# Two fused transformer blocks in split float32: index heads projected first, a LayerNorm moved from GpSimd to VectorE, and several operations put in another order

## The chip, the cores and the metric

The kernel runs on one core of a Trainium2 chip. The metric is the device time of one launch in microseconds. Engines are named as in the profile: PE is TensorE, DVE is VectorE, ACT is ScalarE, POOL is GpSimd, SP is SyncE, which issues the weight loads. The computation has batch 1 and 256 tokens, so each token tensor is two tiles of 128 partitions, tile 0 and tile 1.

## What is computed

The first block runs twice (layers 0 and 1). Each layer projects the input, selects 64 keys for each query with four small index heads, runs eight-head attention on the selected keys, gates a second half through a causal token mix (whose input `v` goes through GELU and a LayerNorm of its own), and then has an output projection, a feed-forward part and a gated side input `p`.

```
h = x @ w_in[i]                        # 1024 x 2116: q k v | qi ki wi | u | vs
logits = einsum('bqhd,bsd->bqhs', qib, ki);  score = einsum(relu(logits), wib)
_, idx = lax.top_k(score, topk)        # 64 of up to 256 keys
b_out = u * (einsum(w, layer_norm(v)) + b_s)       # u, v after gelu
mix = concatenate([a_out, b_out]) @ w_o[i]
x = layer_norm(ALPHA * x + mix, ln1_g[i], ln1_b[i])
ffn = (silu(gate) * up) @ w_ffn_out[i]
ple = (p[i] @ w_ple[i]) * sigmoid(x @ w_ple_gate[i])
x = layer_norm(ALPHA * x + ffn + ple, ln2_g[i], ln2_b[i])
```

The second block also has two layers (an even and an odd one). Each has an RMS norm with a modulation, a large input projection, two kinds of attention, an output projection gated into x, a second RMS norm with modulation, and a squared-ReLU feed-forward part 1024 x 4096 x 1024.

## The kernel before

A hand-written list fixes the order of everything: `do(part, ...)` appends to `order`, and each engine's program walks the same list and emits its own share of each part. So an engine works strictly in the order of that list, and a wait in one part holds up all that comes later on that engine.

All large matmuls are three matmuls of float32r: a weight piece is split into a high half (`high`, a copy on ACT into another buffer of `WB`) and a low half (`low`, a subtraction on DVE, L1728), and activations are split the same way (`XTH`/`XTL`, `HTH`/`HTL`; the low halves are DVE subtractions, L1733, L1795, L1799, L1823). PE computes high x high (L1415), high x low (L1416) and low x high (L1417). A piece holds up to 2048 columns for each partition: four 128-row steps of 512 columns, or of fewer. One piece is used by both token tiles, that is by 24 matmuls when it has four row steps.

`loads` issues the transfers on SP; `advance()` emits `high` and `low` for pieces until three pieces are ready ahead of PE (`cur["pairs"]`), and `advance(1)` for one. With `cur["lag"]` set, `advance` leaves the low half of the newest piece pending; it is emitted at the next `advance`, at the next call of `lows()`, or when its matmul is emitted. `linear` runs one chunk of weights over both tiles; with `touter=True` tile 0 goes through all its pieces first, and `mid()` is called between the tiles. `linear2` runs two chunks A and B (two pieces each) so that tile 1 may come late: A0 and A1 of tile 0, B0 of tile 0, then A0, A1, B0 of tile 1, then B1 of both. Its `mid()` emits what makes tile 1 ready; it is called after A0 of tile 0 (`mid_at=0`).

`busy(b, pad)` (L1400) lets PE run `pad` matmuls of 512 bf16 columns with results that nobody reads, ahead of a wait. They are called filler matmuls here.

The first block's layer, in order: three chunks of 364 columns (`w_in` columns 0 to 1092) are copied to `H` (`hin`). `rope_in` on DVE rotates the index heads and then the q/k heads of each tile, and duplicates the keys into `KD`. PE transposes nine 128-column blocks of each tile (`turn_T`, L1430), `sel_score` computes the index logits (L1452) and DVE adds them up (L1875). Eight rounds of `sel_round` (MAX8 and MATCH_REPLACE8, L1889 and L1892) and `sel_mask` (L1899) follow, with the two GELU chunks between the rounds. `sgu_ln` is the gated half's LayerNorm: sums on ACT, small values on POOL, the normalised value on ACT, and gain and bias on POOL (L1367, L1371). `p_split` splits the side input on ACT and DVE (L1904). Then `attention` runs six units: `scores` (L1491, mask L1497), `soft` (maxima on DVE L1911, L1921, exponentials on ACT), `turns` (transposes of E, L1430) and `values` (L1515), with a filler generator that gives PE other work in between. The output projection, LayerNorm `ln_tile` (`ln_stats` on DVE, `rsqrt` on POOL L1337 and L1339, `ln_apply` of two 128x1024 instructions on DVE, L1991 and L1994), both halves of `w_ple`, and `w_ple_gate` (a `linear2`) follow.

In the second block `norm_tile` is square sums on ACT, `rsqrt` on POOL and `norm_apply` on DVE (L1999). `modulate` (called `go(t, pad)`) is eight PE transposes and scale and shift on ACT and DVE (L1817), and the split into `XTH` and `XTL` (L1823). `gated_put` (L2078, L2082) adds an output chunk to x on DVE.

## Time and profile before

| what | value |
|---|---|
| median of 3 runs | 1409.96 us (1406.32 to 1410.85) |
| the profiled execution | 1406.22 us |
| its span, first to last instruction | 1404.3 us |
| mean granted TensorE clock | 0.985 |
| PE busy | 1317.6 us, 94% |
| DVE busy | 918.9 us, 65% |
| ACT busy | 658.9 us, 47% |
| POOL busy | 110.8 us, 8% |
| HBM traffic in the first fortieth of the span | 371 GB/s |

All times within the execution are microseconds from the start of the span. Busy time of PE contains its filler matmuls and is therefore an upper bound of its useful work. In a row of the timeline the bracket at the end is the idle time of the engine just before the row, and what ended it. Matmuls overlap in the pipeline, so the time of one is read from start to start.

### The profile page before, as it was taken

What the parts mean: (1) busy time and instruction counts of PE and PEld (TensorE: products, weight loads), DVE (VectorE), ACT (ScalarE), POOL (GpSimd) and SP (SyncE); (2) the same over time, 40 slices, a digit from 0 to 9 for tenths busy, and PEclk for the clock granted to TensorE, in tenths of its full rate; (3) what the DMA queues carried; (4) which work ended last, traced back from release to release, by engine and by line L of the source; (5) the groups of instructions that cost most, each with busy time, mean ns of one, the idle gap of its engine ahead of it and who ended that gap; (6) DMA issues with size and microseconds to landing.
All of it is one profiled execution on the core that took longest, in us unless ns stands there. A gap on an engine that the chain in (4) does not pass through costs nothing.

```text
span 1404.3 us, 16099 instructions
## 1 busy us (share of the span) xinstructions
PE 1317.6 (94%) x6462; PEld 1081.6 (77%) x6492; DVE 918.9 (65%) x1225; ACT 658.9 (47%) x886; POOL 110.8 (8%) x157
## 2 busy tenths in 40 slices
PE   6999999999989999999898898999998969999998
PEld 6767888887967788887698776888876857788886
DVE  4857677766675767775666857766666785654444
ACT  5544533443463544343465454554445544554542
POOL 1020000000020000000214200000003320000000
PEclk9999999999999999999998999999999999999999
DMA  9505588873712668885163203776764420465450
GB/s 371 215 1 210 186 317 312 313 287 120 277 61 75 229 241 311 313 313 202 58 207 112 89 32 142 282 298 252 292 232 153 176 91 1 145 213 182 180 180 30
DMA packets 40361, 270.35 MB, mean 193 GB/s; under 512 B 4560, under 2 KB 4560, under 8 KB 12000
## 3 DMA queue, kind: packets, MB, share of 16 engines
q1 hardware_dynamic: 37712, 259.31, 49.8%
q0 software_dynamic: 2432, 8.98, 1.8%
q8 instruction: 51, 0.84, 0.2%
q10 hardware_dynamic: 144, 1.05, 0.2%
q14 instruction: 22, 0.18, 0.0%
HBM read 268.27 MB, written 1.05 MB: 192 GB/s over the span
## 4 chain that ended last, share of the span: by engine, by line
PE 82%; DVE 10%; ACT 3%; issue 2%; POOL 1%; DMA 1%; SPq 0%; POOLq 0%; ACTq 0%; DVEq 0%
PE ps L1415 24%; PE ps L1417 24%; PE ps L1416 24%; PE ps L1430 5%; PE ps L1515 2%; DVE WB L1728 2%; PE ps L1491 1%; PE ps L1400 1%; DMA RAW<-W 1%; ACT WB L1528 1%; DVE st L1981 1%; DVE X L1991 1%; DVE st L1911 1%; DVE X L1994 1%; ACT E L1528 1%
## 5 line engine op out<-in xcount | busy, mean ns | idle before, releaser
L1728 DVE TENSOR_TENSOR WB<-RAW,WB 128x2048 fp32r<-128x2048 f32 (+4 forms) x210 | 453.4, 2162 | 312.9 <-ACT WB L1528 312.4
L1528 ACT ACTIVATE WB<-RAW 128x2048 fp32r<-128x2048 f32 (+4 forms) x210 | 379.9, 1810 | 232.3 <-PE ps L1417 218.2
L1415 PE MATMUL ps<-WB,XTH 128*128 128x512 f32 (+3 forms) x1176 | 455.4, 387 | 19.6 <-DVE XTL L1733 13.1
L1417 PE MATMUL ps<-WB,XTL 128*128 128x512 f32 (+3 forms) x1176 | 447.3, 380 | 0.0
L1416 PE MATMUL ps<-WB,XTH 128*128 128x512 f32 (+3 forms) x1176 | 447.2, 380 | 0.0
L1415 PEld LDWEIGHTS ps<-WB,XTH 128*128 128x128 f32 x1176 | 223.2, 190 | 61.3 <-DVE XTL L1733 13.4
L1417 PEld LDWEIGHTS ps<-WB,XTL 128*128 128x128 f32 x1176 | 222.6, 189 | 38.3
L1416 PEld LDWEIGHTS ps<-WB,XTH 128*128 128x128 f32 x1176 | 223.0, 190 | 35.7
L1415 PE MATMUL ps<-WB,HTH 128*128 128x512 f32 (+1 forms) x452 | 178.8, 396 | 2.5 <-DVE HTL L1799 2.0
L1417 PE MATMUL ps<-WB,HTL 128*128 128x512 f32 (+1 forms) x452 | 178.4, 395 | 0.0
L1416 PE MATMUL ps<-WB,HTH 128*128 128x512 f32 (+1 forms) x452 | 178.3, 394 | 0.0
L1784 DVE CUSTOM_DVE_ANT_0 RAW<-RAW,cond,colv 128x1024 f32<-128x1024 f32 x96 | 119.3, 1280 | 0.0
L1415 PEld LDWEIGHTS ps<-WB,HTH 128*128 128x128 f32 x452 | 85.1, 188 | 23.0 <-DVE HTL L1799 2.4
L1417 PEld LDWEIGHTS ps<-WB,HTL 128*128 128x128 f32 x452 | 85.1, 188 | 20.1
L1416 PEld LDWEIGHTS ps<-WB,HTH 128*128 128x128 f32 x452 | 85.1, 188 | 19.9
L1337 POOL TENSOR_SCALAR st<-st 128x1 f32<-128x1 f32 (+3 forms) x42 | 23.3, 555 | 976.7 <-DVE st L1984 524.7
L1528 ACT ACTIVATE HTH<-ps 128x512 fp32r<-128x512 f32 (+1 forms) x58 | 32.1, 586 | 138.9 <-PE ps L1430 138.7
L1528 ACT ACTIVATE GB<-ps 128x512 f32<-128x512 f32 (+1 forms) x94 | 46.4, 500 | 90.1 <-PE ps L1417 90.1
L1528 ACT ACTIVATE E<-ps,st 128x128 f32<-128x128 f32 (+1 forms) x104 | 42.5, 420 | 74.7 <-DVE st L1921 74.7
L1400 PE MATMUL ps<-cstb 128*128 128x512 bf16 x198 | 57.0, 398 | 1.8 <-issue 0.2
L1799 DVE TENSOR_TENSOR HTL<-ps,HTH 128x512 fp32r<-128x512 f32 x54 | 35.7, 686 | 32.2 <-ACT HTH L1528 32.2
L1339 POOL TENSOR_TENSOR st<-st,cst 128x1 f32<-128x1 f32 (+3 forms) x42 | 48.2, 1147 | 3.5
(175 smaller groups left out, 989.3 us busy)
## 6 DMA issues: line engine op xcount, KB each, us to landing
RAW<-W SPq DMA_DIRECT2D x220, 1024.0 KB, 5.0
RAW<-W SPq DMA_DIRECT2D x14, 768.0 KB, 4.3
RAW<-W SPq DMA_DIRECT2D x12, 728.0 KB, 5.8
VEC<-vecd POOLq DMA_DIRECT2D x10, 512.0 KB, 7.5
RAW<-W SPq DMA_DIRECT2D x8, 512.0 KB, 3.5
RAW<-W SPq DMA_DIRECT2D x4, 576.0 KB, 3.7
GB<-xTd ACTq DMA_DIRECT2D x1, 1024.0 KB, 8.0
X<-xd SPq DMA_DIRECT2D x1, 1024.0 KB, 17.3
```

The lines of the kernel that those rows point to most:

```text
L1337: eng.tensor_scalar(x, x, scale, eps, ALU.mult, ALU.add).then_inc(*own.up())
L1339: eng.tensor_tensor(x, x, MH.to_broadcast([128, x.shape[1]]), ALU.pow).then_inc(*up("rsqrt", key))
L1400: eng.matmul(banks[b][:, :], identb, cstb[:, 0:512], start=True, stop=True)
L1415: eng.matmul(ps, xh, hi[:, j, c0:c0 + cw], start=first and j == 0, stop=False)
L1416: eng.matmul(ps, xh, lo[:, j, c0:c0 + cw], start=False, stop=False)
L1417: op = eng.matmul(ps, xl, hi[:, j, c0:c0 + cw], start=False, stop=last and j == n - 1)
L1430: op = eng.transpose(banks[b][0:rows, j * 128:j * 128 + 128], src, ident)
L1515: op = eng.matmul(banks[b][:, c0:c0 + dv], PET[:, u["i"], blk * 128:blk * 128 + 128], val, start=(j == 0), stop=(j == len(lst) - 1))
L1528: return eng.activation(dst, src, f, **k)
L1728: eng.tensor_tensor(WB[:, it["raw"], 0:w], RAW[:, it["raw"], 0:w], WB[:, it["high"], 0:w].bitcast(F32), ALU.subtract).then_inc(*up("wl", n))
L1784: op = eng.tensor_tensor_reduce(view[:, q, :], view[:, q, :], cond[:, :], 1.0, colv[:, b0:b0 + 1], ALU.mult, ALU.add, modc[:, it["layer"], ...
L1799: eng.tensor_tensor(HTL[:, r2:r2 + 2, :], banks[b][:, :].rearrange("p (n q) -> p n q", n=2), HTH[:, r2:r2 + 2, :].bitcast(F32), ALU.subtra ...
```

## The change

1. The chunks of `w_in` go in another order and widths: the index columns with wi (768 to 1092, 324 wide) first, then `vs` (512), then q/k/v as 384 and 384, then `u` (512). `rope_in` is cut in two: `rope_sel` (index heads) and `rope_qk`. The index heads are transposed after the first piece of `vs`, scored after its second piece, and the selection rounds run beside the q/k/v chunks. `rope_qk` follows the selection.
2. The gated half's LayerNorm: POOL keeps the small values; gain, bias, mean and root are applied by DVE in two `scalar_tensor_tensor` instructions for each tile (`sgu_apply`). ACT's application and POOL's four are gone.
3. `w_ple`'s first half moves into the attention's filler, ahead of the gating, and its result goes to a place of its own (`PLE`). `p_split` moves up between rounds 3 and 4.
4. The `u` chunk and all until the attention is emitted with `lag` set. The first scores come after q/k are transposed; the wait for the first exponentials has 2 filler matmuls in place of 8.
5. `ln_apply` is cut into `ln_scale`, which does not wait for the root, and `ln_shift`. In places another part stands between them (`halfway`).
6. `mid_at=1` in four of the `linear2` calls (`w_ple_gate`, both input projections of the second block, and `mlp_w1_2`): `mid()` comes after A1 of tile 0. In the second block `gated_put` goes ahead of `modulate`, and the low half of the next piece lags behind it. Between the blocks `norm_sums` brings the root of tile 0 forward, and `modulate` stands between scale and shift of tile 1.

```diff
     for i in range(2):
-        all_rows("w_in", i, 1024, (0, 364), (364, 728), (728, 1092), (1092, 1604), (1604, 2116))
+
+        all_rows("w_in", i, 1024, (768, 1092), (1604, 2116), (0, 384), (384, 768), (1092, 1604))
+        all_rows("w_ple", i, 256, halves[0])
         all_rows("w_o", i, 1024, *halves)
-        all_rows("w_ple", i, 256, *halves)
+        all_rows("w_ple", i, 256, halves[1])
...
+        def ln_tile(key, t, after, between=None, before=None, halfway=None):
             sts, mv = col(12), col(2)
             do("ln_stats", key, t, sts, mv, after)
+            if before:
+                before()
             do("rsqrt", ("ln", key), mv[:, 1:2], 1.0, 1e-5, ("ln_mv", key))
             if between:
                 between()
-            do("ln_apply", key, t, mv)
+            do("ln_scale", key, t, mv)
+            if halfway:
+                halfway()
+            do("ln_shift", key, t, mv)
...
+            def put_sel(t, b, done):
+                put_index(t, b, done)
+                if t:
+                    rope_sel(0)
+
             if i:
-                run(linear2("w_in", "x", xt_w, puts[0:2], mid_in, pad=(6, 0)))
+                fill = linear2("w_in", "x", xt_w, [put_sel, put_gelu(1)], mid_in, pad=(6, 0))
             else:
-                run(linear("w_in", "x", xt_w, puts[0], touter=True))
-                run(linear("w_in", "x", xt_w, puts[1]))
-            run(linear("w_in", "x", xt_w, puts[2]))
...
+                run(linear("w_in", "x", xt_w, put_sel, touter=True))
+                fill = linear("w_in", "x", xt_w, put_gelu(1))
+            next(fill)
+            rope_sel(1)
...
+            tws = []
             for t in range(2):
...
+                tws += turn_T([H[:, t, 768 + j * 128:896 + j * 128] for j in range(2)] + [MIX[:, t, 256:384]],
+                              [("kd", (i, t, 2))] + t_pe, 6, t, pad=0 if t else 2)
+            run(fill)
             for t in range(2):
                 do("sel_start", i, t)
...
+            fill = chain(linear("w_in", "x", xt_w, put_in(1, 0, 384)), linear("w_in", "x", xt_w, put_in(2, 384, 768)))
...
             for rnd in range(8):
+                if rnd % 2 == 0:
+                    next(fill, None)
+                if rnd == 4:
+                    do("p_split", i, list(pt_free))
...
+            for t in range(2):
+                do("rope_qk", i, t, hw[t] + mix_free[t], list(scr["free"]))
+                scr["free"] = [("kd", (i, t, 1))]
+            do("sgu_apply", i, mean, root)
...
+            cur["lag"] = True
+            run(linear("w_in", "x", xt_w, put_gelu(0)))
+            tw = []
+            for t in range(2):
+                tw += turn_T([H[:, t, j * 128:j * 128 + 128] for j in range(4)]
+                             + [MIX[:, t, j * 128:j * 128 + 128] for j in range(2)],
+                             [("kd", (i, t, 1))] + t_pe, 0, t, pad=0 if t else 2)
...
             def gating():
-                yield
                 do("sgw_mask", i)
+                yield from linear("w_ple", "p", [[("pl", i)], [("pl", i)]], put_ple(0))
...
+                    if c and t:
+                        x_n[1] = ln_tile((i, 1, 1), 1, rw[1], halfway=lambda: advance(1))
...
-            attention(units, 0.125, fill, pads=(8,), first=8 if i else 3)
+            attention(units, 0.125, fill, first=3)
...
-            run(linear2("w_ple_gate", "x", xt_w, [put_g(0), put_g(1)], mid1, pad=(0, 3)))
+            run(linear2("w_ple_gate", "x", xt_w, [put_g(0), put_g(1)], mid1, pad=(0, 3), mid_at=1))
...
-                    elif t:
-                        norm_tile(0, x_n[0])
-                        go(0, pad=14)
-
-                x_n[t] = ln_tile((i, 2, t), t, [("add_out", (i, t, c)) for c in range(2)], between)
+
+                before = norm_sums(0, x_n[0]) if t and i else None
+                x_n[t] = ln_tile((i, 2, t), t, [("add_out", (i, t, c)) for c in range(2)], between, before,
+                                 (lambda: go(0, pad=14)) if t and i else None)
...
             def put(t, b, done):
+                gput(t, b, done)
                 if t:
                     go(0)
-                gput(t, b, done)
-                if t:
                     advance(1)
                     norm_tile(1, xg[1])
+
+            cur["lag"] = True
             run(linear(nm_out, "x", xo_w, put, touter=True, mid=lambda: norm_tile(0, xg[0])))
+            cur["lag"] = False
+            lows()
...
             def last(t, done):
-                if t and i == 0:
-                    go(0)
                 for c in range(2):
                     gated_put(i, c, 1, xg)(t, acc4[t][c][0], done[c])
+                    if t and c == 0 and i == 0:
+                        go(0)
...
+            def sgu_apply(i, mean, ss):
+                on.wait_ge(*at("vec2", (i, 2)))
+                for t in range(2):
+                    x = GB[:, t, 512:1024]
+                    on.wait_ge(*at("ln_ss", (i, t)))
+                    on.wait_ge(*at("ln_mean", (i, t)))
+                    eng.scalar_tensor_tensor(out=x, in0=x, scalar=mean[t], in1=VEC[:, 2048:2560], op0=ALU.add,
+                                             op1=ALU.mult).then_inc(*up("sgu_g", (i, t)))
...
+            def ln_scale(key, t, mv):
+                xs, n = X[:, t, :], 3 * (key[1] - 1)
+                on.wait_ge(*at("ln_mv", key))
+                on.wait_ge(*at("vec0", (key[0], n)))
+                eng.scalar_tensor_tensor(out=xs, in0=xs, scalar=mv[:, 0:1], in1=VEC[:, 0:1024], op0=ALU.subtract,
+                                         op1=ALU.mult).then_inc(*up("ln_scaled", key))
```

## Rows read from the trace of the kernel before

**Rows 1.** The page: PE's busy time; the chain of waits by engine, shares.
```profile
PE 1317.6 (94%) x6462; PEld 1081.6 (77%) x6492; DVE 918.9 (65%) x1225; ACT 658.9 (47%) x886; POOL 110.8 (8%) x157
...
PE 82%; DVE 10%; ACT 3%; issue 2%; POOL 1%; DMA 1%; SPq 0%; POOLq 0%; ACTq 0%; DVEq 0%
```

**Rows 2.** Timeline of PE, layer 0: start us, us, instruction, [idle before <-releaser].
```profile
19.34 0.43 PE L1415 MATMUL ps<-WB,XTH 128*128 128x364 f32 x1 [0.78 <-DVE XTL L1733]
...
39.45 0.39 PE L1415 MATMUL ps<-WB,XTH 128*128 128x512 f32 x1
...
44.68 0.39 PE L1417 MATMUL ps<-WB,XTL 128*128 128x512 f32 x1
...
70.36 0.72 PE L1491 MATMUL ps<-T 64*128 64x128 f32 x8 [2.71 <-DVE selb L1899]
...
78.21 1.11 PE L1430 MATMUL ps<-cst,E 128*128 128x128 f32 x4 [2.49 <-ACT E L1528]
...
133.20 1.09 PE L1430 MATMUL ps<-cst,X 128*128 128x128 f32 x8 [0.80 <-DVE X L1994]
...
135.40 0.50 PE L1415 MATMUL ps<-WB,XTH 128*128 128x512 f32 x1 [1.11 <-DVE WB L1728]
```

**Rows 3.** Timeline of PE, layer 1, at the same two waits.
```profile
405.18 0.72 PE L1491 MATMUL ps<-T 64*128 64x128 f32 x8 [1.62 <-DVE selb L1899]
...
413.03 1.11 PE L1430 MATMUL ps<-cst,E 128*128 128x128 f32 x4 [4.11 <-ACT E L1528]
```

**Rows 4.** Windows: PE, PEld, DVE, ACT, POOL busy, then PEclk, DMA, GB/s.
```profile
78.00:82.00 4.00, 3.79 (x17) 3.05 (x18) 1.76 (x5) 2.04 (x11) 0.00 (x0) 0.57 0.02 4
66.98:79.32 12.34, 7.07 (x35) 3.87 (x35) 8.55 (x23) 9.66 (x29) 7.82 (x12) 0.82 0.12 43
```

**Rows 5.** Timeline of DVE, first block, layer 0.
```profile
16.48 1.68 DVE L1728 TENSOR_TENSOR WB<-RAW,WB 128x1456 fp32r<-128x1456 f32 x1 [2.13 <-ACT WB L1528]
18.07 1.22 DVE L1733 TENSOR_TENSOR XTL<-GB,XTH 128x1024 fp32r<-128x1024 f32 x1
...
40.85 0.32 DVE L1834 TENSOR_TENSOR SCR<-H,COS 128x160 f32<-128x160 f32 x1
...
42.27 0.24 DVE L1834 TENSOR_TENSOR SCR<-H,COS 128x80 f32<-128x80 f32 x1
...
49.95 1.51 DVE L1875 SCALAR_TENSOR_TENSOR SCR<-E,H,SCR 128x128 f32<-128x128 f32 x4 [1.57 <-ACT E L1528]
...
54.08 0.62 DVE L1889 MAX8 st<-SCR 128x8 f32<-128x128 f32 x2
...
70.07 0.43 DVE L1899 TENSOR_SCALAR selb<-SCR 128x128 bf16<-128x128 f32 x2
...
73.87 1.60 DVE L1904 TENSOR_TENSOR PTL<-T,PTH 128x512 fp32r<-128x512 f32 x1 [3.37 <-ACT PTH L1528]
...
119.58 1.28 DVE L1991 SCALAR_TENSOR_TENSOR X<-X,st,VEC 128x1024 f32<-128x1024 f32 x1 [1.02 <-POOL st L1339]
```

**Rows 6.** Timeline of POOL, second block: one of the rsqrt instructions.
```profile
869.60 0.98 POOL L1337 TENSOR_SCALAR st<-st 128x1 f32<-128x1 f32 x1 [8.48 <-ACT MIX L1528]
```

**Rows 7.** Timeline of DVE at the same moment.
```profile
868.24 2.29 DVE L1728 TENSOR_TENSOR WB<-RAW,WB 128x2048 fp32r<-128x2048 f32 x1
```

**Rows 8.** Timeline of PE at the four norm-and-modulate places of the second block.
```profile
684.58 1.09 PE L1430 MATMUL ps<-cst,MIX 128*128 128x128 f32 x8 [3.31 <-DVE MIX L1999]
...
689.11 0.58 PE L1415 MATMUL ps<-WB,XTH 128*128 128x384 f32 x1
...
694.53 1.10 PE L1430 MATMUL ps<-cst,MIX 128*128 128x128 f32 x8 [2.46 <-DVE MIX L1999]
...
872.06 1.10 PE L1430 MATMUL ps<-cst,MIX 128*128 128x128 f32 x8 [2.34 <-DVE MIX L1999]
...
1066.35 1.09 PE L1430 MATMUL ps<-cst,MIX 128*128 128x128 f32 x8 [3.51 <-DVE MIX L1999]
...
1215.84 1.09 PE L1430 MATMUL ps<-cst,MIX 128*128 128x128 f32 x8 [2.32 <-DVE MIX L1999]
```

More of the change, by code:

```diff
@@ L707, in put_in, with put_gelu, put, rope_sel @@
                 return put
-            puts = [put_in(c, a, b_) for c, (a, b_) in enumerate(((0, 364), (364, 728), (728, 1092)))]
+            gw = [[], []]
+            def put_gelu(c):
+                def put(t, b, done):
+                    do("gelu", (i, c, t), t, c, b, [done] + gb_free)
+                    gw[t].append(("gelu", (i, c, t)))
+                    give(b, ("gelu", (i, c, t)))
+                return put
+            def rope_sel(t):
+                do("rope_sel", i, t, hw[t] + mix_free[t], list(scr["free"]))
+                scr["free"] = [("kd", (i, t, 2))]
@@ L795, in program, with put_ple, put @@
             sgo = ("gated", (i, 1))
+            def put_ple(c):
+                def put(t, b, done):
+                    do("ple", (i, c, t), t, c, b, [done] + pt_free)
+                    give(b, ("ple", (i, c, t)))
+                return put
             rw = [[], []]
@@ L832, in program @@
             xt_w = xt_n
-            for c in range(2):
-                def put(t, b, done, c=c):
-                    do("ple", (i, c, t), t, c, b, [done, sgo])
-                    give(b, ("ple", (i, c, t)))
-                run(linear("w_ple", "p", [[("pl", i)], [("pl", i)]], put))
+            run(linear("w_ple", "p", [[("pl", i)], [("pl", i)]], put_ple(1)))
             def mid1():
@@ L1106, in program @@
                 run(weave(chain(linear2("odd_w_in_2", "x", xt_w, [put_H("odd", c, c * 512, c * 512 + 512, dw[c])
-                                                                  for c in range(2)], mid, pad=(11, 0)), part((3, 4))),
+                                                                  for c in range(2)], mid, pad=(11, 0), mid_at=1), part((3, 4))),
                           [[ch[0, 0][0]], [gs[0], ch[0, 1][0], ch[0, 0][1]], [gs[1], ch[0, 1][1], ch[1, 0][0]],
@@ L1621, in sgu_ln @@
                         ).then_inc(*up("ln_ss", (i, t)))
-                for t in range(2):
-                    on.wait_ge(*at("ln_nb", (i, t)))
-                    act(GB[:, t, 512:1024], GB[:, t, 512:1024], ACT.Identity, bias=nb[t], scale=ss[t]
-                        ).then_inc(*up("ln_x", (i, t)))
             def p_split(i, after):
@@ L1854, in rope_in, with rope_qk @@
                                   ).then_inc(*up("wi", (i, t)))
+            def rope_qk(i, t, after, free_):
+                for e in after + free_:
+                    on.wait_ge(*at(*e))
                 h3 = H[:, t, 0:640].rearrange("p (h d) -> p h d", d=64)[:, :, 0:16]
-                rope(h3.rearrange("p h (a f) -> p h a f", a=2), cs, sn, 10, 8).then_inc(*own.up())
+                rope(h3.rearrange("p h (a f) -> p h a f", a=2), twice(COS[:, t, 0:8]), twice(SIN[:, t, 0:8]), 10, 8
+                     ).then_inc(*own.up())
                 on.wait_ge(*own.at())
@@ L1961, in gating @@
                 on.wait_ge(*at("gating", (i, gh)))
+                for t in range(2):
+                    on.wait_ge(*at("gelu", (i, 0, t)))
                 for gg in range(4):
```

99 lines of the change are left out of this document (37 added, 62 removed).

## The prediction, made before the changed kernel was run

> **What bounds the kernel now.** I read the page first: PE is busy 94% of the span and 82% of the chain of waits, DVE 10% [rows 1]. So the kernel ends when PE has done its matmuls, and another engine costs time only where PE stands. Then I read PE's timeline for places where it waits or runs filler matmuls. Outside the weight matmuls there are about fifty, mostly under a microsecond. The large ones the change touches are these.
>
> - Selection to attention, in both layers of the first block: PE waits 2.71 us for the selection mask and 2.49 us for the first exponentials, besides its filler matmuls [rows 2]; in layer 1 it is 1.62 and 4.11 [rows 3]. The whole stretch from the last projection matmul to the end of the first transposes of E is 12.3 us [rows 4].
> - LayerNorm ahead of `w_ple_gate`: 0.80 and 1.11 us, in layer 0, with as much again in layer 1 [rows 2].
> - The second block's norms: 3.31, 2.46, 2.34, 3.51 and 2.32 us [rows 8].
>
> The clock matters too: in the 4 us after the long stand at the exponentials it was granted 0.57 [rows 4], so 1.2 GHz for most of that stretch, which about doubles the matmul time in it.
>
> PE's weight work stays. Three chunks of 364 become 324 + 384 + 384, again 1092 columns and the same number of matmuls. A piece of 512-column matmuls takes 5.5 us: 24 of them, 5.23 us from the first start to the last [rows 2], or 0.228 us each. For 324 and 384 columns I scale that by columns with a small fixed part: about 0.150 and 0.175 us each, so 3.6 and 4.2 us for a piece of 24.
>
> **The first block, part by part.**
>
> *Start of layer 0.* Tile 1's low half is queued on DVE behind the low half of the third piece, 1.68 us, and takes 1.22 [rows 5]; PE starts tile 1 at 19.34 [rows 2]. The third piece is now `vs` with 2048 columns: low half 1.68 x 2048/1456 = 2.36 (+0.6), its high half on ACT about +0.5, and 136 KB more to load before it, 0.4 us at the 371 GB/s of this part of the span. PE starts tile 1 some 1.5 us later.
>
> *Index heads.* PE must wait for `rope_sel` of tile 1 after only one `vs` piece. That rope stands on DVE behind a low half of 2048, the rope of tile 0 and a low half of 1536. One 2048 low half is 2.29 [rows 7], 1536 scales to 1.7; the q/k rope of ten heads takes 1.42 from start to start [rows 5], the index one of five heads with its copies at most that, I take 1.0. So 2.3 + 1.0 + 1.7 + 1.0 = 6.0 us, of which the `vs` matmuls (2.7 us in layer 1's order, up to 5.5 in layer 0) and the time until the high half is made cover a part. I price 2.5 us per layer; the bounds are 0 and 5.
>
> *Selection.* Beside it PE now has q/k/v and `u`: 4 x 4.2 + 2 x 5.5 = 27.8 us, and 1.9 for 12 transposes and 2 filler matmuls. On DVE stand: adding the logits 54.08 - 49.95 = 4.1; the eight rounds, 70.07 - 54.08 = 16.0 less the three low halves between them (6.9), 9.1; mask 0.4; four low halves 2 x 1.7 + 2 x 2.3 = 8.0; `p_split`, 1.60 in its row, which I take as 0.7 (below); `rope_qk` 2.8 [rows 5]. That is 25.1: the q/k transposes don't wait. Then `sgu_apply`, four instructions of 512 columns, half of a 1.28 us one each [rows 5], 2.7 with gaps, a low half of `w_ple` (1.2) and DVE's copy of the transposed q/k (0.7). DVE ends at 29.7 + about 0.5 for the relu, PE at 29.7 + copy. A wait of about 1.5 us before the first scores is left, mostly inside the 3 filler matmuls.
>
> By the timelines laid side by side, the first scores of layer 0 then start at about 71.5 where they started at 70.36: the start (1.5), the index wait (2.5) and the copy (1.5) eat the 3.4 us of the mask wait and the 1.5 us of fillers, 1.1 later net. In layer 1, without the start, they come at the same 405.2. What is won is behind them: 8.96 us from scores to the end of the first transposes (70.36 to 79.32) become scores 1.1, scores 1.1, two fillers 0.5 and transposes 0.5 = 3.2, with `w_ple`'s 12 matmuls (2.7, moved, counted below) as cover for the exponentials. That is 5.8, and about 1.1 more because the slow stretch behind it goes. DVE has two low halves and the mask of the mixing weights (1.2) ahead of the second maxima; I take 1.0 off for it. Net: layer 0 5.8 + 1.1 - 1.0 - 1.1 = 4.8; layer 1 5.9.
>
> *Taking 2.7 us of `w_ple` from the stretch ahead of `w_ple_gate`.* It covered DVE's work on LayerNorm. The 0.80 and 1.11 us waits and 0.7 of fillers go, but A1 of tile 0 now needs a low half that lies between `ln_scale` and `ln_shift`, and 4 filler matmuls stand ahead of the transposes without use. I come to 2.0 us regained of the 2.7: -0.7 per layer.
>
> *`ln_scale` ahead of the root.* Before, DVE stood 1.02 us for POOL's root [rows 5]. But a POOL instruction that usually takes 0.19 took 0.98 and ended at 870.58, just after the DVE subtraction of two SBUF operands ended at 870.53 [rows 6, 7]. `ln_scale` has two SBUF operands as well and starts at the moment POOL wants to start. So POOL's root slides behind it and `ln_shift` waits: I count 0 for the split, with 0.95 at each of six LayerNorm tiles on PE's path as the upper bound. The Trainium skill, "SBUF — State Buffer", section "SBUF: two separate sides", says the same as a rule: the port pair shared by VectorE and GpSimd is locked for a whole instruction, by a VectorE one with two SBUF inputs as well. By the rule the split gives nothing where it stands alone; without it the sum would be 3 to 5 us better. It is also why I take `p_split` at 0.7: in its row POOL's gain and bias ran beside it, and they are gone.
>
> **The second block.** A `linear2` with `mid_at=1` covers tile 1's norm with A1 (2.7 us at 512 columns, 2.1 at 384), but leaves only B0 (2.7; 1.6 for 288 columns) between the transposes and A0 of tile 1; that path takes about 3.3 us (689.11 - 684.58 less 1.1 of transposes is 3.4 [rows 8]), so some 0.6 comes back.
> - Between the blocks: tile 0's root no longer stands behind that of tile 1; its transposes start about 1.8 earlier, and without the 3.31 us stand no fillers at half clock follow. With tile 1: 2.4 us won.
> - Even layer's feed-forward: `gated_put` first and the low half deferred bring the norm of tile 1 forward about 1.5, but the deferred low halves and two 1.28 us modulation sums now stand ahead of tile 1's split. DVE becomes the bound: 0.4 won.
> - Odd layer's input: 2.2. Odd feed-forward, the same without the modulation sums: 2.4.
>
> **Sum.** 4.8 + 5.9 - 1.4 + 2.4 + 0.4 + 2.2 + 2.4 = 16.7 us against a span of 1404.3 (device time 1406.22 with 1.9 around it). The work was laid out by hand without the hops between engines at the new waits, so I take 15. The profiled execution lies 0.3% under the median; I subtract from the median: 1409.96 - 15 = 1395.0 us.
>
> **Rivals.**
> - *As computed*, 1389 to 1400: chance 0.55.
> - *DVE binds at more places than the one*: the index wait is nearer 5 than 2.5 in each layer, and the low halves deferred in the second block stand in front of the splits at three places rather than one. Costs 5 + 3: 7 won, 1403. For it: DVE is already the releaser of nearly every wait of PE. Against: it idles about a third of the span [rows 1]. 0.18.
> - *The lock doesn't hold, and slow-clock stretches go that I left standing*: split 4 us, clock 3 to 6: 1385 to 1388. Of the clock: a stand of 2.49 us was followed by a slow stretch [rows 2, 4], and transposes and fillers behind the 3.31 us stand took 4.5 us [rows 8]; small shifts can go either way. 0.10. The split alone would give 1395 - 4 = 1391, which counts with the first case. That would go against the rule of the Trainium skill's page named above.
> - *Within 0.3%*: the pieces cancel, as the first scores already do: start 1.5, index wait 5, no gain from the norms. 1409.96 - 3: 1407. 0.10.
> - *Slower*: with `lag`, low halves are emitted right behind the maxima of a unit and ahead of the next unit's. In each of the 12 units of the two attentions the exponentials could be 2.3 us late and PE with them, up to 27 us. It decides from 1.6 us a unit on, where it has eaten the 19 us beyond which the time is slower by more than 0.3%; full size 1420. Against: the attention had `lag` before, and only two more low halves fall into it. 0.07.
>
> **Range and chances.** 1384 to 1408 holds the first four cases and cuts most of the last and the outer part of the others. About 0.3% (4.2 us) is what a measurement can tell from no change. Faster by more: 0.55 + 0.18 + 0.10 = 0.83 less a little for the tail of the second, 0.82; within 0.11; slower 0.07. The first case's own range is 1389 to 1400.
>
> **What would show it.** After: no wait for `selb` and only a short one for E at the first unit; PE standing 2 to 3 us at the transposes of the index heads (MIX or H from DVE) in both layers; tile 1 starting near 21 rather than 19.34; `ln_shift` following `ln_scale` with a gap of about a microsecond, and the POOL scaling lengthened to over 1 us beside `ln_scale`; in the second block transposes without a wait for L1999's instruction, but short waits for XTL after B0. The prediction is wrong if the index wait exceeds 5 us, if waits for E appear at the later units, or if new slow stretches stand where the clock was full.

## The result: 24.7 us won, 15 forecast

| kernel | median us | runs | profiled execution | span | clock |
|---|---|---|---|---|---|
| before | 1410.24 | 1406.32 to 1410.85 (4) | 1406.22 | 1404.3 | 0.985 |
| changed | 1385.53 | 1384.38 to 1386.78 (4) | 1386.78 | 1385.0 | 0.984 |

The ratio is 0.9831, 95% interval 0.981 to 0.9852. The forecast was 1395.0 with a range of 1384 to 1408 and 0.82 on faster. The time lies in the range, below the first case's own 1389 to 1400.

The two traces differ by 19.3 us of span, the two medians by 24.7. The 5 us between are no row's: before was profiled at the lower end of its runs (1406.22, median 1410.24), the changed kernel at the upper end of its own. What the sum forecast is to be held against 19.3, and the sum was 16.7. (Below, PE "stands" where it waits, and a stretch is "at half clock" where the granted clock is near 0.5, that is 1.2 GHz. The forecast had 0.55 on 1389 to 1400; 1385.5 lies 3.5 us below that.)

First the page of the changed kernel: busy times, then the chain of waits by engine.

```profile
PE 1313.3 (95%) x6436; PEld 1079.2 (78%) x6467; DVE 921.2 (67%) x1233; ACT 654.2 (47%) x882; POOL 110.8 (8%) x145
...
PE 82%; DVE 11%; ACT 3%; issue 2%; DMA 1%; POOL 1%; SPq 0%; DVEq 0%; ACTq 0%; POOLq 0%
```

Beside [rows 1] no engine's busy time moved by more than 5 us. PE has 26 instructions fewer, all of them fillers (198 before, 172 after). The span became 19.3 us shorter and PE's busy time 4.3: for the most part PE stands less. Where, the timeline of PE tells. Layer 0 of the first block:

```profile
20.80 0.64 PE L1445 MATMUL ps<-WB,XTH 128*128 128x324 f32 x1 [2.62 <-DVE XTL L1759]
...
32.34 0.44 PE L1460 MATMUL ps<-cst,H 128*128 128x128 f32 x2
...
70.36 0.71 PE L1521 MATMUL ps<-T 64*128 64x128 f32 x8 [0.18 <-issue]
...
75.40 0.60 PE L1460 MATMUL ps<-cst,E 128*128 128x128 f32 x4
...
126.77 0.77 PE L1445 MATMUL ps<-WB,XTH 128*128 128x512 f32 x1 [2.60 <-DVE WB L1754]
...
131.85 1.04 PE L1460 MATMUL ps<-cst,X 128*128 128x128 f32 x8
```

Neither the mask nor the exponentials are waited for. The first scores start at 70.36, to the hundredth where they started in [rows 2]; the end of the first transposes of E is 76.00, after 79.32, with the 12 matmuls of `w_ple` done on the way. In return a wait of 2.60 us stands at 126.77, where 0.80 and 1.11 stood. Layer 1 (beside [rows 3]):

```profile
358.51 0.44 PE L1460 MATMUL ps<-cst,H 128*128 128x128 f32 x2 [0.35 <-DVE MIX L1877]
...
361.15 0.44 PE L1460 MATMUL ps<-cst,H 128*128 128x128 f32 x2 [2.10 <-DVE MIX L1877]
...
400.77 0.71 PE L1521 MATMUL ps<-T 64*128 64x128 f32 x8 [0.18 <-issue]
```

And the second block, to be read beside [rows 8]:

```profile
672.49 1.09 PE L1460 MATMUL ps<-cst,MIX 128*128 128x128 f32 x8 [0.72 <-DVE MIX L2052]
...
679.68 0.41 PE L1445 MATMUL ps<-WB,XTH 128*128 128x384 f32 x1 [1.20 <-DVE WB L1754]
...
686.00 0.41 PE L1445 MATMUL ps<-WB,XTH 128*128 128x384 f32 x1 [1.06 <-DVE XTL L1849]
...
863.24 0.47 PE L1445 MATMUL ps<-WB,XTH 128*128 128x512 f32 x1 [0.96 <-DVE XTL L1849]
...
1048.45 0.47 PE L1445 MATMUL ps<-WB,XTH 128*128 128x512 f32 x1 [1.19 <-DVE WB L1754]
```

Of the five waits of 2.3 to 3.5 us for `norm_apply` one of 0.72 is left. A short one for a low half (WB) or a split (XTL) stands in the place of the others, 5.1 us in all for 13.9.

Reading the start of the same matmul in both timelines gives the account by stages. "Won" is what the distance grew by within the stage. "Gate stretch" is all from the output projection `w_o` on: LayerNorm, `w_ple`, `w_ple_gate` and the feed-forward part up to its output transposes; what changes in it lies around `w_ple_gate`.

| stage, to the start of | before | after | won | forecast |
|---|---|---|---|---|
| layer 0, `w_o` | 105.01 | 100.68 | 4.3 | 4.8 - 2.7 = 2.1 |
| layer 0 gate stretch, to the output transposes | 331.78 | 326.23 | 1.2 | 2.0 |
| layer 1, first scores | 405.18 | 400.77 | -1.1 | 0 |
| layer 1, `w_o` | 439.68 | 431.10 | 4.2 | 5.9 - 2.7 = 3.2 |
| layer 1 gate stretch | 666.36 | 656.87 | 0.9 | 2.0 |
| between the blocks | 718.95 | 705.88 | 3.6 | 2.4 |
| even feed-forward (848.59 to 835.30 at its head) | 1044.44 | 1029.29 | 1.9 | 0.4 |
| odd input | 1112.84 | 1095.73 | 2.0 | 2.2 |
| odd feed-forward | 1388.21 | 1368.86 | 2.2 | 2.4 |

They sum, with 0.2 in the stage ahead of the even feed-forward's head, to 19.3. The 2.7 is `w_ple`'s half, done in the attention and missing behind it.

### The profile page after: what moved, and what is told of

Its sections match the earlier page's. It is cut to its first block, busy times and chain, and to the rows that moved or that the text cites. A ratio compares the mean times of both kernels' runs of the same rounds, so it can differ in the third digit from the quotient of the medians.

```text
span 1385.0 us, 16064 instructions
## 1 busy us (share of the span) xinstructions
PE 1313.3 (95%) x6436; PEld 1079.2 (78%) x6467; DVE 921.2 (67%) x1233; ACT 654.2 (47%) x882; POOL 110.8 (8%) x145
## 4 chain that ended last, share of the span: by engine, by line
PE 82%; DVE 11%; ACT 3%; issue 2%; DMA 1%; POOL 1%; SPq 0%; DVEq 0%; ACTq 0%; POOLq 0%
PE ps L1445 24%; PE ps L1447 24%; PE ps L1446 24%; PE ps L1460 4%; DVE WB L1754 2%; PE ps L1545 2%; PE ps L1521 2%; PE ps L1430 1%; DMA RAW<-W 1%; ACT WB L1558 1%; DVE st L2030 1%; DVE st L1958 0%; DVE SCR L1860 0%; DVE XTL L1821 0%; PE ps L1527 0%
## 5 line engine op out<-in xcount | busy, mean ns | idle before, releaser
L1378 POOL TENSOR_SCALAR st<-st 128x1 f32<-128x1 f32 (+3 forms) x42 | 28.5, 680 | 981.3 <-DVE st L2033 533.8
L1558 ACT ACTIVATE GB<-ps 128x256 f32<-128x256 f32 (+1 forms) x86 | 42.0, 488 | 94.0 <-PE ps L1447 93.9
L1380 POOL TENSOR_TENSOR st<-st,cst 128x1 f32<-128x1 f32 (+3 forms) x42 | 52.9, 1259 | 3.5
L1430 PE MATMUL ps<-cstb 128*128 128x512 bf16 x172 | 48.7, 382 | 1.8 <-issue 0.2
```

Of the source, the lines that this page charges most:

```text
L1378: eng.tensor_scalar(x, x, scale, eps, ALU.mult, ALU.add).then_inc(*own.up())
L1380: eng.tensor_tensor(x, x, MH.to_broadcast([128, x.shape[1]]), ALU.pow).then_inc(*up("rsqrt", key))
L1430: eng.matmul(banks[b][:, :], identb, cstb[:, 0:512], start=True, stop=True)
L1558: return eng.activation(dst, src, f, **k)
```

## The experiments

Twelve kernels, all variants of the changed one. Their waits are read from their own traces; lines differ by one or two from those above.

**1. The split of LayerNorm undone in effect.** `ln_scale` waits for the root, as the joined function did.

```diff
             def ln_scale(key, t, mv):
-                on.wait_ge(*at("ln_mv", key))
+                on.wait_ge(*at("rsqrt", ("ln", key)))
```

> The changed kernel with ln_scale waiting for POOL's root again, as ln_apply did; the root is then computed while DVE stands. Lock theory (POOL cannot read beside a DVE instruction with two SBUF operands): the split gives only 0.3 us a tile, since after it POOL's scaling took 1.20 to 1.28 us and ln_shift still stood 0.72 us. Joining costs 0 to 2 us: 1386 to 1388. Rival (the split was worth its full 0.95 us at four to six tiles, and is where the unforeseen gain came from): 4 to 6 us slower, 1390 or more.

Measured: 1392.44 (1390.74 to 1393.18), ratio 0.9881 [0.9862, 0.9899]; the span is 6.4 us above that of the changed kernel. My theory of next to nothing missed the size; the rival's 1390 or more came. The lock itself is there. This is DVE of the changed kernel at the two LayerNorm tiles of layer 0:

```profile
114.00 0.21 DVE L2033 BATCH_NORM_AGGREGATE st<-st 128x2 f32<-128x12 f32 x1
114.25 1.29 DVE L2039 SCALAR_TENSOR_TENSOR X<-X,st,VEC 128x1024 f32<-128x1024 f32 x1
116.25 1.29 DVE L2047 SCALAR_TENSOR_TENSOR X<-X,st,VEC 128x1024 f32<-128x1024 f32 x1 [0.72 <-POOL st L1380]
...
123.14 1.29 DVE L2039 SCALAR_TENSOR_TENSOR X<-X,st,VEC 128x1024 f32<-128x1024 f32 x1
124.34 2.28 DVE L1754 TENSOR_TENSOR WB<-RAW,WB 128x2048 fp32r<-128x2048 f32 x1
127.07 1.28 DVE L2047 SCALAR_TENSOR_TENSOR X<-X,st,VEC 128x1024 f32<-128x1024 f32 x1 [0.44 <-POOL st L1380]
```

POOL at the same time:

```profile
114.38 1.20 POOL L1378 TENSOR_SCALAR st<-st 128x1 f32<-128x1 f32 x1 [52.34 <-DVE st L2033]
115.67 0.55 POOL L1380 TENSOR_TENSOR st<-st,cst 128x1 f32<-128x1 f32 x1
123.19 1.28 POOL L1378 TENSOR_SCALAR st<-st 128x1 f32<-128x1 f32 x1 [6.97 <-DVE st L2033]
124.56 2.48 POOL L1380 TENSOR_TENSOR st<-st,cst 128x1 f32<-128x1 f32 x1
```

POOL's 0.19 us instruction takes 1.20 and ends as `ln_scale` does; its 0.55 us one takes 2.48 beside the low half. In the experiment POOL takes 0.19 and 0.55 again, and DVE stands 1.03 us for it. From the end of the statistics to the end of the shift tile 0 needs 3.57 us in the changed kernel (113.97 to 117.54) and 3.95 in the experiment (115.01 to 118.96). So the split is worth 0.4 a tile by itself. What I had not seen is that the low half for A1 stands *between* scale and shift at the second tile: with the split it follows a scale that did not wait. That gives 0.9 more, at each gate stretch; with the low half in another place (experiment 8) this part was not measured. The experiment's rows of PE:

```profile
119.02 1.09 PE L1460 MATMUL ps<-cst,X 128*128 128x128 f32 x8 [0.69 <-DVE X L2047]
...
129.10 0.57 PE L1445 MATMUL ps<-WB,XTH 128*128 128x512 f32 x1 [3.51 <-DVE WB L1754]
...
461.15 0.76 PE L1445 MATMUL ps<-WB,XTH 128*128 128x512 f32 x1 [3.52 <-DVE WB L1754]
```

Laid against the changed kernel PE falls back 1.0 at 25 us (half clock there for longer, ahead of any LayerNorm), 0.4 at 119.02, 0.9 at 129.10, 0.5 ahead of layer 1's projection (and comes 0.3 nearer in it), 0.6 and 0.9 at the LayerNorms behind its attention, 1.3 of half clock behind the 3.52 stand, then 0.3 and 0.4 between the blocks and 0.3 behind them. Some 4 us are the edit's, 2.3 the clock's, of which the 1.3 stand behind a wait that the edit had lengthened. Here the Trainium skill ("SBUF — State Buffer", section "SBUF: two separate sides") and the trace agree on the mechanism: POOL is held for the length of a VectorE instruction with two SBUF inputs (1.20 for 0.19). My inference from it, that the split then gives nothing, was wrong.

**2. The first half of `w_ple` put back behind `w_o`** (weights order, the filler in the attention and the loop after it as before).

```diff
-                yield from linear("w_ple", "p", [[("pl", i)], [("pl", i)]], put_ple(0))
+                yield
...
-            run(linear("w_ple", "p", [[("pl", i)], [("pl", i)]], put_ple(1)))
+            for c in range(2):
+                run(linear("w_ple", "p", [[("pl", i)], [("pl", i)]], put_ple(c)))
```

> The changed kernel with w_ple's first half behind the output projection again. Theory of the prediction: it covers the exponentials of the first unit, so PE stands about 2.5 us more there in each layer and a slow-clock stretch may follow; but ahead of w_ple_gate it covers DVE, where 2.6 us of waiting go. Net 0.7 us a layer better to 2 us a layer worse: 1384 to 1390. Rival (the place in the attention is what the gain comes from): 4 us a layer slower, 1393.

Measured: 1390.83 (1388.4 to 1392.49), ratio 0.9872 [0.9853, 0.9891]. PE at the first unit:

```profile
70.48 0.72 PE L1521 MATMUL ps<-T 64*128 64x128 f32 x8 [0.68 <-DVE T L1817]
...
74.00 0.66 PE L1460 MATMUL ps<-cst,E 128*128 128x128 f32 x4 [1.08 <-ACT E L1558]
75.79 1.16 PE L1492 MATMUL ps<-GB,T 128*128 128x128 f32 x8 [1.13 <-DVE T L2003]
```

The changed kernel starts that last matmul at 75.83. With 2.7 us less work PE is no earlier: those 12 matmuls lie wholly in the time in which E and T are made. Behind the attention the 2.7 comes back as work, and the half ahead of the gate takes 0.6 of it by shortening the 2.60 wait (to 1.88): 2.15 us later at the output transposes of layer 0. In layer 1's attention it is only 0.9 later (407.15 for 406.25), since a stretch at half clock near 365 was absent, and 2.5 at the output transposes of layer 1; at the end the spans differ by 1.6. The medians differ by 5.3: the profiled execution took 1388.40, the low end of its runs, the changed kernel's 1386.78, the high end. So the median lies 0.8 above the theory's interval and 2.2 below the rival's time, and the trace accounts for only a part of it.

**3. The gate branch's LayerNorm by ACT and POOL again.** `sgu_apply` goes; ACT scales and shifts, POOL applies gain and bias.

```diff
-            do("sgu_apply", i, mean, root)
...
+                    act(GB[:, t, 512:1024], GB[:, t, 512:1024], ACT.Identity, bias=nb[t], scale=ss[t]
+                        ).then_inc(*up("ln_x", (i, t)))
```

> The changed kernel with the gated half's LayerNorm applied by ACT and POOL again. POOL's four instructions and ACT's two then end only about 8 us after the sums, that is near 68 us in layer 0 where the gating needs it at about 76: nothing waits, and DVE has 2.8 us less ahead of the q/k copies. Prediction's accounting: no more than 1 us either way, 1384.5 to 1387. Rival (the move to DVE is the gain, because POOL's reads lock DVE out): rope_qk and the splits beside POOL's instructions get longer and the first scores come 2 or more us later in each layer, 1390 or more.

Measured: 1387.52 (1385.89 to 1389.49), ratio 0.985 [0.9832, 0.9868], whose interval overlaps that of the changed kernel. The first scores are 0.75 later, with a wait of 0.79 for DVE's copy of T; by the output transposes of layer 0 that is made up, and the spans are equal (1385.1 and 1385.0). But it was made up by the clock: behind the 2.61 us wait at the gate (127.55) it was granted 1.00, where the changed kernel had 0.63 behind its 2.60. In layer 1 the first scores lose 0.9 again. The median is 2.0 above the changed kernel's and 0.5 above the expected interval, and the runs overlap. So moving this norm to DVE may be worth 1 to 2 us; this measurement can't tell that from nothing.

**4. All edits of the second block and between the blocks undone.**

> The changed kernel with everything in the second block and between the blocks undone (mid_at=0 in its three calls, modulate ahead of gated_put, no lag, old order of tile 1's LayerNorm). By the anchors of the two traces the part between and in the second block won 3.6 + 1.9 + 2.0 + 2.2 = 9.7 us: 1395. The prediction had 7.4: 1393. Rival (slow-clock stretches did it, so that the parts don't add up): under 1390 or over 1400.

Measured: 1398.61 (1395.71 to 1399.95), ratio 0.9926 [0.9906, 0.9945]; span 8.9 above the changed kernel's. The old waits are back, four of the five within 0.01 of [rows 8] and the first at 2.70 for 3.31 (the fifth is 2.32, at 1205.41):

```profile
674.09 1.10 PE L1459 MATMUL ps<-cst,MIX 128*128 128x128 f32 x8 [2.70 <-DVE MIX L2051]
...
684.03 1.09 PE L1459 MATMUL ps<-cst,MIX 128*128 128x128 f32 x8 [2.45 <-DVE MIX L2051]
...
861.57 1.09 PE L1459 MATMUL ps<-cst,MIX 128*128 128x128 f32 x8 [2.33 <-DVE MIX L2051]
...
1055.85 1.09 PE L1459 MATMUL ps<-cst,MIX 128*128 128x128 f32 x8 [3.52 <-DVE MIX L2051]
```

So about half of the gain stands in the second block. In the traces the two halves add up: 9.7 won there, 8.9 lost by undoing it, and by the same stages 1.9, 2.1 and 2.2 for the last three (1.9, 2.0, 2.2 in the table). The median is another matter: it rose by 13.1 and lies 3.6 above the 1395 expected; the profiled execution, 1395.71, was again at the low end.

**5. `mid_at=1` undone at its four calls.**

```diff
-            run(linear2("w_ple_gate", "x", xt_w, [put_g(0), put_g(1)], mid1, pad=(0, 3), mid_at=1))
+            run(linear2("w_ple_gate", "x", xt_w, [put_g(0), put_g(1)], mid1, pad=(0, 3)))
```

(and so at `even_w_in_2`, `odd_w_in_2` and `mlp_w1_2`)

> The changed kernel (1385.5 us) with one thing undone: all four linear2 calls again cover tile 1's norm with nothing but what stands before A1 (mid_at 0 instead of 1). Theory: A1 of tile 0 is the cover of tile 1's norm, so PE must stand again for DVE's norm at the transposes of tile 1 of the second block, about 2 us at each of four places (waits of the size of the 3.31, 3.51 and 2.46 us before the change less what the other edits took off), and in the gate stretch of both layers the half ahead of A1 no longer stands for its low half: 6 to 9 us lost, 1392 to 1395 us. Rival: the earlier norm alone (sums ahead of the root, gated_put first) had done the work and the order of A1 counts for little: loss under 3 us, below 1389.

Measured: 1390.45 (1388.02 to 1392.41), ratio 0.9866 [0.9839, 0.9892]. The theory had 1392 to 1395, the rival below 1389: neither; the waits are of the theory's kind, though one of them is 0.87, and the sum is smaller. Its rows of PE:

```profile
128.44 1.97 PE L1460 MATMUL ps<-cst,X 128*128 128x128 f32 x8 [3.37 <-DVE X L2047]
...
683.59 1.97 PE L1460 MATMUL ps<-cst,MIX 128*128 128x128 f32 x8 [2.16 <-DVE MIX L2052]
...
860.78 1.09 PE L1460 MATMUL ps<-cst,MIX 128*128 128x128 f32 x8 [0.87 <-DVE MIX L2052]
...
1054.03 1.09 PE L1460 MATMUL ps<-cst,MIX 128*128 128x128 f32 x8 [2.15 <-DVE MIX L2052]
```

Much of each stand is only exchanged for the shorter waits for WB and XTL. Net, by the stages of the table, PE falls back 1.9 and 0.7 in the two gate stretches, 1.2 between the blocks, nothing in the even feed-forward (0.4 ahead of its head), 0.6 at the odd input and 0.9 in the odd feed-forward.

**6. The feed-forward order undone** (modulation ahead of `gated_put`, no deferred low halves, and the last half of layer 0 in the old order).

```diff
-                gput(t, b, done)
                 if t:
                     go(0)
+                gput(t, b, done)
+                if t:
                     advance(1)
                     norm_tile(1, xg[1])
-            cur["lag"] = True
             run(linear(nm_out, "x", xo_w, put, touter=True, mid=lambda: norm_tile(0, xg[0])))
```

> The changed kernel with only the feed-forward edits of the second block undone: gated_put after the modulation of tile 0, no deferred low halves, and in the last half of layer 0 the modulation before both sums. Theory: these forecast 0.4 us where they won 1.9 in the even feed-forward; without them 1 to 3 us are lost, 1386.5 to 1388.5 us, and a wait of PE of 1 us or more comes back at the transposes of tile 1 in the even and odd feed-forward. Rival: all of the gain of 1.9 and 2.2 us came from mid_at, then the time stays at 1384 to 1387 with no new wait.

Measured: 1387.07 (1386.16 to 1388.02), ratio 0.9842 [0.9819, 0.9866]: in the theory's interval, but the measurement can't tell 1.5 us from none. In the trace A0 of tile 0 starts 1.06 later in the even feed-forward (853.38), of which 0.39 is older, but tile 1's A0 only 0.31 (863.55): nothing is lost by then. In the odd input A1 waits 2.52 for its low half where it waited 1.19, and 1.4 is lost. The wait forecast at tile 1's transposes did not come back. So the even feed-forward's 1.9 belongs to neither edit alone: undoing the order costs nothing there, undoing `mid_at` (experiment 5) costs nothing there, and undoing both (experiment 4) costs 1.9 and brings the wait of 2.33 back. Either one covers the norm. At the odd input both together cost 2.1, `mid_at` alone 0.6 and the order alone 1.4.

**7. Tile 1's low half first, at the start of layer 0.**

```diff
             do("x0", 0)
-            advance()
+            advance(1)
             do("x0", 1)
+            advance()
```

> One thing added to the changed kernel: at the start of layer 0 the low half of tile 1 is emitted ahead of the low half of the 2048-column third piece, so that PE does not wait 2.62 us for it at 20.80. Theory (the step of the prediction that priced the start at 1.5): the wait of 2.62 us goes, the matmuls behind it no longer run at half clock, the first scores come 1.5 to 3 us before 70.36, and the time is 1382.5 to 1384 us. Rival: PE then waits for the low half of the third piece or for its load instead, and nothing is won: within 1 us of 1385.5.

Measured: 1386.61 (1385.4 to 1388.96), ratio 0.9843 [0.9813, 0.9873]: no gain, and 0.1 us outside the rival's interval. The wait of 2.62 went and PE was 4.3 us ahead at 24 us. Then:

```profile
29.09 0.41 PE L1461 MATMUL ps<-cst,H 128*128 128x128 f32 x2 [1.44 <-DVE MIX L1878]
...
31.65 0.69 PE L1461 MATMUL ps<-cst,H 128*128 128x128 f32 x2 [2.04 <-DVE MIX L1878]
```

and its windows (us, then the busy time of PE, PEld, DVE, ACT, POOL, the granted clock, DMA):

```profile
28.00:32.00 4.00, 0.87 (x5) 0.66 (x6) 3.53 (x14) 0.49 (x1) 0.00 (x0) 0.77 1.03 414
32.00:36.00 4.00, 4.00 (x12) 3.23 (x11) 1.52 (x1) 3.15 (x3) 0.00 (x0) 0.50 1.01 410
```

PE ran into the ropes of the index heads, stood 3.5 us, and was granted 0.50 behind that, 1.2 GHz. At 37 us it was 1.75 *behind* the changed kernel. That its span ends 0.7 us earlier all the same comes from layer 1, where two stretches at half clock were absent (1.00 behind the waits at 363.17 and 457.56). A stand that is merely moved can return with its half-clock stretch and cost more than it did.

**8. The low half for A1 ahead of tile 1's LayerNorm**, rather than in its middle.

```diff
-                        x_n[1] = ln_tile((i, 1, 1), 1, rw[1], halfway=lambda: advance(1))
+                        advance(1)
+                        x_n[1] = ln_tile((i, 1, 1), 1, rw[1])
```

> One thing changed: the low half for A1 of w_ple_gate is made ahead of the LayerNorm of tile 1 and not between its scale and its shift, in both layers. Theory: the 2.60 us wait of PE for that low half goes (126.77 and 457.19), the norm of tile 1 comes 1.2 us later and shows as a wait of under 1.5 us at its transposes; net 1 to 2 us per layer, 1382 to 1384 us. Rival: the transposes of tile 1 are the bound of the stretch anyway, the wait only moves behind them: within 1 us of 1385.5.

Measured: 1382.24 (1381.64 to 1382.53), ratio 0.9808 [0.9784, 0.9831]. The median lies in the theory's interval, with all runs below those of the changed kernel. The wait of 2.60 is gone; in its stead, in layer 0 and alike in layer 1:

```profile
128.60 1.09 PE L1461 MATMUL ps<-cst,X 128*128 128x128 f32 x8 [0.78 <-DVE X L2048]
130.80 0.79 PE L1446 MATMUL ps<-WB,XTH 128*128 128x512 f32 x1 [1.11 <-DVE WB L1755]
```

The stretch at half clock behind the 2.60 goes too in layer 1 (0.57 in 457 to 461 us of the changed kernel, 1.00 in 455 to 459 of this one). In layer 0 it moves behind 130.80 (0.60 in 130 to 134), and of the 1.9 us that PE is ahead there 0.3 are left at 135 us. Of the 4.3 us between the two spans, 2.1 are won in layer 1's gate stretch; 1.6 come ahead of layer 1's attention, a place that the edit doesn't touch. PE stands there for the index heads as before, but at full clock:

```profile
360.97 0.44 PE L1461 MATMUL ps<-cst,H 128*128 128x128 f32 x2 [2.10 <-DVE MIX L1878]
```

```profile
360.00:364.00 4.00, 3.03 (x15) 2.55 (x16) 1.47 (x8) 2.43 (x3) 0.00 (x0) 1.00 0.96 401
```

So one trace shows about 2 us a layer for the order itself, as forecast, before the clock; two short stands were cheaper than a long one in layer 1 and hardly so in layer 0.

**9 to 12, on one chip, five rounds:** the changed kernel again as control; both ropes ahead of the low half; that with experiment 8; all three.

```diff
                 if t:
                     rope_sel(0)
+                    rope_sel(1)
...
             next(fill)
-            rope_sel(1)
```

> The changed kernel as it is, once more, on the chip of the next three, so that they are compared with it on one chip. Expected: 1385.5 us within 2 us.

> One thing changed: the rope of tile 1's index heads is emitted right behind that of tile 0, ahead of the 1536-column low half of the next piece, in both layers. Theory (the step of the prediction that priced the index wait at 2.5 us a layer): in layer 1 PE stands 2.1 us at 361.15 because that low half lies ahead of the rope; the wait goes and 1 to 2 us are won there; layer 0, whose start sets the pace, wins nothing. 1383.5 to 1384.5 us. Rival: the low half that is now later is waited for instead, in both layers, and the time is the control's within 1 us or above it.

> The low half ahead of tile 1's LayerNorm and the two ropes together. The first alone gave 1382.2 us beside 1385.5. Theory: both act at places of their own, so the gains add, 3.3 and 1 to 2: 1380 to 1381.5 us. Rival: PE's lead from the ropes is taken away before the attention by DVE, which has the same work in total: 1382 us, as with the first alone.

> All three: tile 1's low half first at the start, both ropes together, and the low half ahead of tile 1's LayerNorm. With the first alone PE stood 1.44 and 2.04 us at the index transposes of layer 0, was granted half the clock behind them, and was 1.75 us later at 37 us than in the changed kernel, although it had been 4.30 us ahead at 24. Theory: with the ropes together the second stand (2.04) goes, and with it the stretch at half clock; then what the start wins is kept at least in part: 1377 to 1380 us. Rival: DVE binds the whole of layer 0's start up to the first scores, and what PE wins at 20 it stands later, with another stretch at half clock: 1380 to 1383 us, not below the version without the first edit.

| kernel | median us | range | ratio to before |
|---|---|---|---|
| control | 1385.46 | 1385.2 to 1386.61 | 0.9838 [0.9821, 0.9855] |
| ropes together | 1383.37 | 1381.55 to 1383.64 | 0.9817 [0.98, 0.9835] |
| with the low half ahead of LayerNorm | 1378.41 | 1378.22 to 1379.24 | 0.9788 [0.9771, 0.9805] |
| all three | 1377.75 | 1376.9 to 1378.67 | 0.9782 [0.9765, 0.9799] |

The control came as expected, the second within 0.2 of its interval, the third beat its theory by 1.6, the fourth is in its theory's interval. In layer 1 the control waits so:

```profile
359.46 0.44 PE L1460 MATMUL ps<-cst,H 128*128 128x128 f32 x2 [2.10 <-DVE MIX L1877]
```

Its window behind that:

```profile
360.00:364.00 4.00, 4.00 (x13) 3.10 (x12) 1.90 (x2) 3.15 (x3) 0.00 (x0) 0.57 0.73 306
```

With the ropes together the wait is down to 0.56 us:

```profile
359.55 0.44 PE L1460 MATMUL ps<-cst,H 128*128 128x128 f32 x2 [0.56 <-DVE MIX L1877]
```

and the same window is at full clock:

```profile
360.00:364.00 4.00, 4.00 (x19) 3.31 (x19) 3.12 (x3) 3.75 (x4) 0.00 (x0) 1.00 1.00 418
```

Against the first trace of the changed kernel, which came to tile 0's index transposes at the same time (358.51, here 358.44), PE is 1.6 ahead at tile 1's and 3.2 at the first scores: 1.6 for the wait and 1.6 for the clock. Against the control's trace it is 1.5, since the control had run at 1.00 in 126 to 130 us and this kernel at 0.57. Layer 0 gains nothing. The two edits together give 7.05, more than the 2.1 and the 3.3 of either alone (the 3.3 across two chips). Of the span's 7.1, 5.9 are there by 461 us, and two of the stretches at half clock that went are in it. All three gain 0.66 more in medians, with overlapping runs; at the first scores they are 1.5 us ahead of two edits, of which 1.4 is left at 461 and 0.7 at the end. The stand at the index transposes is down to one of 2.06, but 0.57 is still granted in 28 to 32 us. Against before the last kernel is 31.7 us faster, 1377.75 to 1409.47.

## Why the forecast held in its direction, and where its sum was off

- *Start of layer 0.* Tile 1 starts at 20.80 for 19.34, 1.46 later for a forecast of 1.5. Right.
- *Index wait, 2.5 a layer.* In layer 1 0.35 + 2.10 = 2.45. Right. In layer 0 there is none in the profiled execution, because PE came later (0.57 granted in 20 to 24 us); in the control, granted 1.00 in that stretch, it stood 1.48 there. The two are alternatives, and I had added them: the first scores of layer 0 came at 70.36 for about 71.5. The sum there was also wrong in itself: 1.5 + 2.5 + 1.5 less 3.4 and 1.5 is 0.6, not 1.1, and the mask wait is 2.71 in its row, not 3.4.
- *Layer 1's first scores unchanged.* 1.1 lost. I had left out the clock behind the index wait: 0.73 and 0.84 in 360 to 368 us, where before had 1.00. Experiment 10 shows it: without most of the wait, and without the stretch, PE is 3.2 us ahead at the first scores, half of it the clock's, though tile 0's transposes come no earlier. The stretch is in part luck: experiment 8 has the same wait at full clock, and does this stage 1.6 us faster.
- *The exponential stand, 5.8 and a slow stretch.* Right: from the first scores to the end of the first transposes of E 5.6 us with `w_ple`'s 2.8 inside, so 2.8 for a forecast of 3.2; the clock is 1.00 in 78 to 82 us after 0.57 [rows 4]. The 1.0 that I took off for DVE's low halves did not come: no wait at the second unit. With the 1.1 of the first scores this makes most of the 4.3 for 2.1 at `w_o`.
- *Gate stretch, -0.7 a layer.* The mis-sized term: -1.5 and -1.8 (1.2 and 0.9 regained of 2.7). The low half between scale and shift keeps PE standing 2.60 and half-clocked behind it. I had priced no wait there. Experiment 8 gives back 1.9 in layer 0, of which the clock takes 1.6 again, 2.1 in layer 1, and 3.3 us in medians.
- *The split, 0.* Wrong: about 4 us (experiment 1). Some 1.8 of it (0.9 in each gate stretch) hang on the low half that stands between scale and shift. The rival "the lock doesn't hold, and the split gives 4" has the right size for the split, and its 1385 to 1388 even holds the measured 1385.5, by the wrong mechanism. The lock holds.
- *Second block, 7.4.* It gave 9.7, by undoing it 8.9 of span. Right in the odd layer (2.0 and 2.2 for 2.2 and 2.4). Between the blocks 1.2 more, the split's share among it. In the even feed-forward DVE was to bind: the two modulation sums do stand ahead of tile 1's split, but PE waits only 0.96 for it, so 1.9 was won for 0.4. Experiments 4, 5 and 6 together show why no term of the sum fits: either `mid_at` or the new order of `gated_put` covers this norm, and one of the two would have done.
- *`p_split` at 0.7.* 0.69 in its row (DVE at 53.90).
- *The rival that DVE binds at more places* fell: DVE does set the new short waits of the second block (0.72 + 1.20 + 1.06 + 0.96 + 1.19 = 5.1), but they are what is left of 13.9. *Lagged low halves delaying the exponentials* fell outright: no new wait for E at any later unit of the first block.
- *One of the signs of being wrong came*: "new slow stretches stand where the clock was full". 20 to 24 us was granted 0.57 and 360 to 368 us 0.73 and 0.84, each 1.00 before, and behind the two waits of 2.60 it was 0.63 and 0.57. The sum has no term for them; that it came out 2.6 short all the same is because the split, the second block and the first scores gave more than forecast.

The haircut from 16.7 to 15 went the wrong way, and the subtraction from the median rather than from the profiled execution put 3.7 us on it. The distance of medians (24.7, and 24.0 with the control) is larger than that of the spans (19.3 and 20.8), and this goes with the granted clock. Of the 23 runs of before that list a clock beside experiments 1 to 12, the 8 at 0.985 or 0.986 took 1405 to 1407 us, as its profiled one did, and the 15 at 0.978 to 0.984 took 1408.8 to 1412.5. My estimate from these: 0.981 rather than 0.985 over 1404 us is 5.6 us of full clock lost. The changed kernel and the control ran at 0.984 to 0.987. Which stretches of before those at 0.981 have at half clock stays open: its one trace is of an execution at 0.985.

## What to carry to other kernels

Put a short piece of work that the bounding engine needs first (here one low half of 2.28 us) ahead of a norm chain rather than into its middle: moving it by one place won 3.3 us here. When a stand is removed, follow PE to the next engine's due time before counting the gain; it is kept only if what comes next is ready (in the traces, experiment 7 against 12). When two edits cover the same wait, undo both as well as each: in the even feed-forward each alone seemed worth nothing. Price a stand together with the stretch at half clock that may follow it: between nothing (behind 3.28 us in the control) and 2.4 us (behind 2.04 in experiment 7).

## What the runs showed of the hardware that was not expected

The half clock behind a stand is not fixed by the program. The control and the changed kernel are one program; the control stood longer at the start and lost nothing:

```profile
20.49 0.42 PE L1445 MATMUL ps<-WB,XTH 128*128 128x324 f32 x1 [3.28 <-DVE XTL L1759]
```

Its window there:

```profile
20.00:24.00 4.00, 3.51 (x23) 3.51 (x24) 3.28 (x14) 1.04 (x4) 0.00 (x0) 1.00 1.01 425
```

while the changed kernel's first execution, behind 2.62 us, was granted less:

```profile
20.00:24.00 4.00, 3.20 (x12) 3.21 (x13) 3.59 (x14) 0.97 (x3) 0.00 (x0) 0.57 1.01 422
```

The wait of 2.10 us in layer 1 shows it over more traces. It stands in ten of them (the changed kernel, the control, experiments 1 to 8), and in the 4 us from the matmul behind it the granted clock was 0.58 to 0.66 in six and 1.00 in four (experiments 2, 4, 7 and 8). In the three traces where that wait is 0.56 us it was 1.00 each time. Differences of 1 to 2 us between two single traces can be this alone, and several of the stage figures above carry it. Second, POOL is held by DVE's low halves as well as by LayerNorm's instructions: 2.48 us for a root that takes 0.55, ending 0.42 us after the low half beside it.
